# The second layer's output projection and feed-forward on 514 tokens, its down-projection on 512, in place of 528

## The reference

```python
h = jnp.concatenate([meta, x], axis=1)                       # 528 tokens
for l in range(DEPTH):                                       # DEPTH = 2
    h = h + hybrid_mixer(rmsnorm(h, norm_mix_g[l]), ...)     # ends in merged @ w_out[l], 1024 x 1024
    h = h + conv_glu_ffn(rmsnorm(h, norm_ffn_g[l]), ...)
return rmsnorm(h, final_norm_g)[:, N_META:]                  # 512 tokens

def conv_glu_ffn(h, w_up, conv_w, conv_b, w_down):
    u = causal_dwconv(h @ w_up, conv_w, conv_b)              # width 3: tokens t, t-1, t-2
    gate, val = jnp.split(u, 2, axis=-1)                     # 2816 each
    return (jax.nn.silu(gate) * val) @ w_down
```

## Time and profile before

| what | us |
|---|---|
| median of 3 runs | 3546.7 |
| the three runs | 3545.86, 3546.7, 3555.61 |
| the profiled execution, its own time | 3553.56 |
| its span, first to last instruction | 3551.8 |
| PE busy | 3449.5 |
| DVE / ACT / POOL busy | 1669.5 / 1174.3 / 1339.3 |

### The profile page before, as it was taken

One profiled execution on the slowest core, in us unless ns is written; L12 is line 12 of the kernel. 1 busy time (PEld: TensorE's weight loads), 2 busy tenths in 40 slices (PEclk: granted clock), 3 DMA queues, 4 the chain that ended last, 5 costly groups with the idle time before them and its releaser, 6 DMA issues.

```text
span 3551.8 us, 55467 instructions
## 1 busy us (share of the span) xinstructions
PE 3449.5 (97%) x20718; PEld 3021.4 (85%) x20718; DVE 1669.5 (47%) x2618; ACT 1174.3 (33%) x1986; POOL 1339.3 (38%) x530
## 2 busy tenths in 40 slices
PE   7998999989989999999999989999999999999999
PEld 6998999989989999888877768888888877888887
DVE  5475534544755345542446654245433533734241
ACT  2464323224643233222235532222222234322122
POOL 3212443423124434344432224444444433344443
PEclk9999999999999999999999989999999999999999
DMA  3212233322122333233322112333232322233333
GB/s 107 72 43 60 87 90 89 93 67 66 43 60 83 95 89 93 79 100 90 97 80 60 54 54 89 98 91 100 86 98 88 103 86 78 83 90 95 94 94 95
DMA packets 570042, 294.86 MB, mean 83 GB/s; under 512 B 10664, under 2 KB 568359, under 8 KB 569783
## 3 DMA queue, kind: packets, MB, share of 16 engines
q1 hardware_dynamic: 568724, 291.33, 28.0%
q0 software_dynamic: 768, 1.11, 0.1%
q10 hardware_dynamic: 418, 0.62, 0.1%
HBM read 290.93 MB, written 2.10 MB: 83 GB/s over the span
## 4 chain that ended last, share of the span: by engine, by line
PE 61%; issue 27%; POOL 7%; DVE 3%; ACT 2%; POOLq 0%; DMA 0%; SPq 0%; ACTq 0%; DVEq 0%
PE big L2094 51%; POOL wlow L727 7%; PE big L2499 3%; PE big L2135 2%; PE misc L2148 1%; PE misc L2159 0%; PE misc L2548 0%; DVE mix_lev L1598 0%; PE misc L2185 0%; DVE fresh L1574 0%; ACT whigh L741 0%; PE misc L2660 0%; PE misc L2267 0%; PE big L2582 0%; DMA load_xin<-in_x 0%
## 5 line engine op out<-in xcount | busy, mean ns | idle before, releaser
L727 POOL TENSOR_TENSOR wlow<-raw,whigh 128x1024 fp32r<-128x1024 f32 (+1 forms) x508 | 1329.1, 2617 | 2180.6 <-ACT whigh L741 2180.6
L741 ACT CAST whigh<-raw 128x1024 fp32r<-128x1024 f32 (+1 forms) x508 | 563.8, 1110 | 1984.5 <-PE big L2094 1803.5
L2094 PE MATMUL big<-ffn_x2l,whigh 128*128 128x264 f32 (+1 forms) x2016 | 540.1, 322 | 0.0
L2094 PE MATMUL big<-ffn_x2h,whigh 128*128 128x264 f32 (+1 forms) x2016 | 537.5, 321 | 2.1 <-DVE ffn_zg L1510 2.1
L2094 PE MATMUL big<-ffn_x2h,wlow 128*128 128x264 f32 (+1 forms) x2016 | 538.8, 322 | 0.0
L2094 PE MATMUL big<-xhigh,whigh 128*128 128x512 f32 (+1 forms) x1680 | 527.8, 352 | 0.7 <-POOL wlow L727 0.7
L2094 PE MATMUL big<-xlow,whigh 128*128 128x512 f32 (+1 forms) x1680 | 520.5, 347 | 0.0
L2094 PE MATMUL big<-xhigh,wlow 128*128 128x512 f32 (+1 forms) x1680 | 518.3, 346 | 0.0
L2094 PE MATMUL big<-ffn_hidl,whigh 128*128 128x264 f32 (+1 forms) x1408 | 421.8, 340 | 0.0
L2094 PE MATMUL big<-ffn_hidh,wlow 128*128 128x264 f32 (+1 forms) x1408 | 421.2, 340 | 0.0
L2094 PE MATMUL big<-ffn_hidh,whigh 128*128 128x264 f32 (+1 forms) x1408 | 419.4, 339 | 0.0
(11 more groups left out here) (407 smaller groups left out, 4111.0 us busy)
## 6 DMA issues: line engine op xcount, KB each, us to landing
raw<-in_ffn_w_gate_up SPq DMA_DIRECT2D x176, 512.0 KB, 3.7
raw<-in_ffn_w_down SPq DMA_DIRECT2D x96, 704.0 KB, 4.6
raw<-in_ffn_w_up SPq DMA_DIRECT2D x88, 512.0 KB, 3.7
raw<-in_w_in SPq DMA_DIRECT2D x52, 512.0 KB, 3.8
raw<-in_gmlp_w_in SPq DMA_DIRECT2D x32, 512.0 KB, 4.0
raw<-in_attn_w_in SPq DMA_DIRECT2D x24, 512.0 KB, 3.6
raw<-in_w_out SPq DMA_DIRECT2D x16, 512.0 KB, 4.0
raw<-in_gmlp_w_out SPq DMA_DIRECT2D x16, 512.0 KB, 3.9
```

Source lines behind the costliest of these rows:

```text
L727: eng.tensor_tensor(wlow[:, at0:at0 + n], raw[:, at0:at0 + n], whigh[:, at0:at0 + n].bitcast(F32), ALU.subtract).then_inc(slab_split, 1)
L741: eng.copy(whigh[:, at0:at0 + w], raw[:, at0:at0 + w]).then_inc(high_rounded, 1)
L2094: mm = eng.matmul(wide(big, slot, T)[:, c:c + n], w[:, (s * KC + k) * P:(s * KC + k + 1) * P], x[:, (x0 + k) * width + c:(x0 + k) * width ...
```

## The change

- A third token count, TE = 514, that is 512 and the two tokens ahead of them. The norm of n = 3, and with it the up-projection, the scaling, ScalarE's squares and VectorE's low parts, run on 514.
- The output projection of the second layer's mixer computes the last 514 tokens; the mixer itself stays on 528.
- Of the convolution's results only the last 512 are written (`drop` = 2 columns are left out), and the product, its two parts, the down-projection and the add to `h` run on K = 512.
- `parts(514)` gives 258 and 256 columns, and `wide` starts at PSUM column 254 of 1024. For 528 both are as before.
- `blocks`, `by_block` and `row_spread` take the first block's width from T (2 columns in place of 16).
- The first layer has T = K = 528 and drop = 0.

```diff
+TE = SEQ + 2
...
         def blocks(T):
 
-            if T == T1:
-                return [(0, 0, META)] + [(t, t, P) for t, _ in CHUNKS[1:]]
-            return [(t, t, P) for t in range(0, T, P)]
+            m = T - T2
+            return [(0, 0, m)] * (m > 0) + [(t, t, P) for t in range(m, T, P)]
...
-            T = T1 if n < 4 else T2
+            T = T1 if n < 3 else TE if n == 3 else T2
...
         def wide(ps, slot, T):
-            at0 = slot * 1024 + (BANK - T1 // 2 if T == T1 else 0)
+            at0 = slot * 1024 + (BANK - parts(T)[0][1] if T > T2 else 0)
             return ps[:, at0:at0 + T]
 
         def parts(T):
-            return [(0, T // 2), (T // 2, T // 2)] if T == T1 else [(0, T)]
+            first = T // 2 + T // 2 % 2
+            return [(0, first), (first, T - first)] if T > T2 else [(0, T)]
+
+        def kept(n):
+            return T1 if n < 3 else T2
...
             def ffn(n, ph):
-                T = T1 if ph[0] == "cffn" else T2
+                T, drop = norm_T[norm_of[n]], norm_T[norm_of[n]] - kept(n)
...
-                            eng.activation(zg[:, :], wide(big, 0, T), ACT.Identity, bias=pdyn("ffn_conv_b", l, f),
+                            eng.activation(zg[:, drop:T], wide(big, 0, T)[:, drop:T], ACT.Identity, bias=pdyn("ffn_conv_b", l, f),
...
-                            eng.activation(sg[:, :], zg[:, :], ACT.Silu).then_inc(silu_ready, 1)
+                            eng.activation(sg[:, drop:T], zg[:, drop:T], ACT.Silu).then_inc(silu_ready, 1)
...
                 conv = ph[0] == "cffn"
-                T = T1 if conv else T2
+                T, K = norm_T[norm_of[n]], kept(n)
+                lo1, lo2, drop = max(1, T - K), max(2, T - K), T - K
...
-                                    out=z[:, 1:T], in0=y[:, 0:T - 1],
-                                    scalar=pdyn("ffn_conv_w", l, 2 * NF + s * NF + f), in1=z[:, 1:T],
+                                    out=z[:, lo1:T], in0=y[:, lo1 - 1:T - 1],
+                                    scalar=pdyn("ffn_conv_w", l, 2 * NF + s * NF + f), in1=z[:, lo1:T],
...
-                        eng.tensor_tensor(pr[:, 0:T], sg[:, 0:T], val, ALU.mult).then_inc(prod_ready, 1)
+                        eng.tensor_tensor(pr[:, 0:K], sg[:, drop:T], val, ALU.mult).then_inc(prod_ready, 1)
                         eng.wait_ge(prod_ready, first + i + 1)
-                        eng.tensor_copy(c1(hidh, i, T), pr[:, 0:T]).then_inc(hidh_ready, 1)
+                        eng.tensor_copy(c1(hidh, i, K), pr[:, 0:K]).then_inc(hidh_ready, 1)
...
-                    residual(down, n, tile0 + 2 * HF, T, scale=None if conv else 0.5, last=half == 1)
+                    residual(down, n, tile0 + 2 * HF, K, scale=None if conv else 0.5, last=half == 1)
...
-                residual(wout, n, t0 + MIX_TILES, T1)
+                residual(wout, n, t0 + MIX_TILES, T1 if l == 0 else TE)
...
-                    plain_pair(down, tile0, 0, T, hidh, hidl, before=lambda k: eng.wait_ge(hid_ready, first + k + 1))
-                    repeat(eng, 1, KD // 2, lambda i: plain_pair(down, tile0, i, T, hidh, hidl))
+                    plain_pair(down, tile0, 0, K, hidh, hidl, before=lambda k: eng.wait_ge(hid_ready, first + k + 1))
+                    repeat(eng, 1, KD // 2, lambda i: plain_pair(down, tile0, i, K, hidh, hidl))
...
+                To = T1 if l == 0 else TE
...
-                            for c, cn in parts(T1):
-                                mm = eng.matmul(wide(big, s, T1)[:, c:c + cn],
+                            for c, cn in parts(To):
+                                mm = eng.matmul(wide(big, s, To)[:, c:c + cn],
                                                 w[:, (s * KC + k) * P:(s * KC + k + 1) * P],
-                                                x[:, k * T1 + c:k * T1 + c + cn],
+                                                x[:, k * T1 + T1 - To + c:k * T1 + T1 - To + c + cn],
```

More of the change, by code:

```diff
@@ L243, in blocks @@
         def blocks(T):
-            if T == T1:
-                return [(0, 0, META)] + [(t, t, P) for t, _ in CHUNKS[1:]]
-            return [(t, t, P) for t in range(0, T, P)]
+            m = T - T2
+            return [(0, 0, m)] * (m > 0) + [(t, t, P) for t in range(m, T, P)]
         def by_block(bank, slot, T):
-            at0 = slot * 1024 + (496 if T == T1 else 0)
+            at0 = slot * 1024 + (BANK + T2 - T if T > T2 else 0)
             return bank[:, at0:at0 + T]
@@ L832, in body @@
                                 eng.wait_ge(prod_ready, first + i)
-                            eng.activation(zu[:, :], wide(big, 1, T), ACT.Identity,
+                            eng.activation(zu[:, drop:T], wide(big, 1, T)[:, drop:T], ACT.Identity,
                                            bias=pdyn("ffn_conv_b", l, NF + f),
@@ L1510, in body @@
                                 eng.scalar_tensor_tensor(
-                                    out=z[:, 2:T], in0=y[:, 0:T - 2], scalar=pdyn("ffn_conv_w", l, s * NF + f),
-                                    in1=z[:, 2:T], op0=ALU.mult, op1=ALU.add).then_inc(tile_out[s], 1)
+                                    out=z[:, lo2:T], in0=y[:, lo2 - 2:T - 2], scalar=pdyn("ffn_conv_w", l, s * NF + f),
+                                    in1=z[:, lo2:T], op0=ALU.mult, op1=ALU.add).then_inc(tile_out[s], 1)
                             eng.wait_ge(tile_out[1], tile0 // 2 + i + 1)
-                            val = zu[:, :]
+                            val = zu[:, drop:T]
                         else:
@@ L1525, in body @@
                             eng.wait_ge(hid_ready, first + i)
-                        eng.tensor_tensor(pr[:, 0:T], sg[:, 0:T], val, ALU.mult).then_inc(prod_ready, 1)
+                        eng.tensor_tensor(pr[:, 0:K], sg[:, drop:T], val, ALU.mult).then_inc(prod_ready, 1)
                         eng.wait_ge(prod_ready, first + i + 1)
-                        eng.tensor_copy(c1(hidh, i, T), pr[:, 0:T]).then_inc(hidh_ready, 1)
+                        eng.tensor_copy(c1(hidh, i, K), pr[:, 0:K]).then_inc(hidh_ready, 1)
                         eng.wait_ge(hidh_ready, first + i + 1)
-                        eng.tensor_tensor(c1(hidl, i, T), pr[:, 0:T], c1(hidh, i, T).bitcast(F32),
+                        eng.tensor_tensor(c1(hidl, i, K), pr[:, 0:K], c1(hidh, i, K).bitcast(F32),
                                           ALU.subtract).then_inc(hid_ready, 1)
```

## The result

| | before | after |
|---|---|---|
| median, 20 runs each | 3552.58 | 3543.86 |
| the profiled execution | 3553.56 | 3544.16 |
| its span | 3551.8 | 3542.4 |

The account below looks back on a forecast made before the run. TensorE's matmul pace was taken to bound the changed stages. Savings of 5.4 us (down-projection) and 7.7 (output and up-projection), less 0.1 for waits, make 13.0 us, from the median 3546.7 to 3533.7, range 3529.5 to 3543.

Parts of the forecast that it names:

- What bounds the stage: Second layer's changed stages: TensorE's matmul pace sets the time, no other engine is over 55% there.
- The down-projection: 16 slabs of 33 pairs of 264 columns become single matmuls of 512, saving 5.4 us.
- What doesn't count: Waits at the up-projection's start cost 0.1 us; VectorE, ScalarE, DMA and weight splitting neither cost nor save.
- the wait for `opl`: In the output projection TensorE waits 2.88 us; the wait starts earlier and keeps its length.
- The seam: Up- to down-projection: slack before the last hidden tile shrinks from 0.33 to 0.15 us, no wait counted.
- the price of the pair of 258 and 256 columns: Output projection and up-projection: 1248 pairs save 6.2 ns each, 7.7 us, between bounds of 0 and 15.4.
- The line's slope: Matmul price through the measured 528 and 512 columns: 0.442 ns a column, beside 5.2 ns a matmul.
- rival (c): Uneven SBUF and PSUM starts cost TensorE cycles; 5.2 ns a matmul cancels the gain, 12 ns gives 3564; chance 0.04.
- Rival (a): Weight loads pace the short matmuls, so only the down-projection gains: 5.4 us, 3541.3; chance 0.14.
- Rival (b): At the seam VectorE's cast meets GpSimd's subtraction, TensorE waits about 2 us twice: gain 9.3 us, 3537.4; chance 0.05.
- the three runs that I started from: Starting time of the whole kernel: median 3546.7 us of three runs lying within 9.8 us.

Follow-up runs that it names:

- the first two experiments: The change with 256 columns cut first, then the change with the second feed-forward's normed input stored 14 columns further: 3540.01 and 3541.31 us (before 3547.07).

## Why the prediction was right and wrong

**Right.** *What bounds the stage.* PE's pace, and nothing else: the gain sits in the stretch, and no engine became a new bound. *The down-projection*, "528 times (242.4 - 232.2) = 10.2 ns, 5.4 us": 5.4 us by the pace, 5.1 in the run that does this alone. *What doesn't count*: the first layer kept its 11.75 and 16.0, the wait for `opl` kept 2.88 us. *The seam*: the term of nothing holds in size, with 0.07 us lost in each half, but "I count no wait" does not: the 0.15 us of slack was not there, and PE's weight load waited 0.23 us in each half.

**Wrong.** The step that failed is the price of the pair of 258 and 256 columns, "Fourteen columns are then 6.2 ns ... 1248 times 6.2 ns is 7.7 us". It was drawn as a line per column through 528 and 512. Measured is a pair at 241.7 ns instead of 237.8, so 2.3 ns saved and not 6.2 in the up-projection, and 3.4 us instead of 7.7 for the whole term. That PE's pace sets the gain was right; the size of this term was off, because the price went by columns alone. The line's slope is not what failed: 4 columns at 0.442 ns are 1.77 ns, and the rule's 4.25 cycles a piece are 1.77 ns too (both rest on the 512-column price). But 528 and 512 columns from aligned bytes are 132 and 128 whole pieces, and no point between them was in the trace; 514 columns cut at byte 1032 are 130 pieces, not the 128.5 that the line puts in. By the rule these 1.5 pieces are 2.7 of the 3.9 ns. The other 1.2 ns stay open: the change, at byte 1032, lies 3.5 cycles over the rule, other cuts into 130 pieces lie up to 3 under it. What needs no rule is that the same 514 columns, read from bytes 0 and 1024 or 56 and 1088, took 238.3 ns, 0.5 ns from the forecast.

**The argument that failed** is in rival (c): "the bytes read per column are the same, and nothing in the trace depends on place". The second half was true of a trace that has aligned starts only, so it said nothing on uneven ones. Rival (c) named the right bytes (1032, a multiple of 8 only) with the wrong size and sign of the outcome: it needs 5.2 ns a matmul to cancel the gain, and the cut costs 1.7 (8 cycles a pair, between 580 and 572). PSUM's column 254, its other half, costs nothing that shows.

**Rival (a)**, that the weight load paces the matmuls, fell with the first two experiments, although its picture, a full weight-load column, is still there: the same column stands full at 11.44, 11.60 and 11.76 us. The Trainium skill ("TensorE: Matmul & The Clock Gate", section "Wait — 56ns, not 53.3ns?") has a pair's price in columns and 2.5 ns a matmul. Of 514 columns it would say one price; the runs show 238.3 to 241.7 ns for the same 514, by where they start. **Rival (b)**, a wait of 2 us at the seam, didn't come about: the cast took 0.43 us there.

**The level.** 5.9 of the 10.2 us between forecast and median come from the three runs that I started from; with the measured gain taken from them, 3538.0, the time would have been in the range, and so it would with the forecast gain taken from the median of 20, 3539.6. I had seen that two of four executions lay 8 to 10 us over the lowest, and gave the high ones too little room.

## What to carry to other kernels

Columns alone don't give a matmul's price: where its moving operand is read from counts too. When a token count is cut down, look where the cut and the start fall, and try a border between the two matmuls at a multiple of 16 bytes (four float32 columns), by the split or by where the tensor is stored: the four kernels of 514 tokens with such a border took 572 to 573.3 cycles a pair, the five others 573.3 to 580. A line through two points that are both aligned says nothing of an uneven one; when a case is new in that respect, the range should hold it. And where runs scatter by more than the gain, read the gain from distances inside the trace, over the stretch that changed.

## What the runs showed of the hardware that I had not expected

- The same 514 columns take 572 to 580 cycles a pair, and 520 columns 574.7 to 588, depending on the bytes at which the two matmuls start to read. Single matmuls of 512 show it too (556 from byte 0, 561 from byte 8). What in the chip makes the place count no run shows.
- Identical code runs at two paces: the up-projection on 528 tokens shows 584 cycles a pair in one half and 587.3 in the other, also where only the down-projection was changed; in the first layer three of the runs with unchanged code there have the first half at 584, the others at 587.3. Matmuls of 512 from bytes 24 and 56 differ between their halves by 3 and 5 cycles as well. This stays unexplained; it is as large as what the rule leaves over.
